# Expert blocks of a mixture-of-experts kernel: the down projection as three rounded products, ScalarE's and VectorE's order rewritten, row numbers copied ahead on GpSimd

## The chip, the cores and the metric

One core of one Trainium2 chip runs the whole program. The time is the device time of one launch in microseconds (us); the kernel's figure is the median of its runs.

## What is computed

One layer of a diffusion backbone on 1152 tokens of width 1024: an mLSTM and a gated linear recurrence, an output projection, and then a mixture of 64 small SwiGLU experts with 8 experts per token and one shared expert. Only this last part is touched. Cut to what matters:

```python
# 9216 (token, expert) entries sorted by expert, each expert padded to blocks of 128 rows
def expert_block(args):
    tok, e = args                      # 128 row numbers, one expert
    xb = x2d[tok]                      # (128, 1024)
    hb = jax.nn.silu(xb @ exp_w1[e]) * (xb @ exp_w3[e])     # (128, 256)
    return hb @ exp_w2[e]              # (128, 1024), the down projection

routed = jax.ops.segment_sum(yb * slot_w, slot_tok, num_segments=N)   # rows added back
shared = (jax.nn.silu(x2d @ shared_w1) * (x2d @ shared_w3)) @ shared_w2
return routed + shared
```

## The kernel before

`stage_experts` runs one loop over blocks of 128 rows. Blocks 0 to 8 (NSH = 9) are the shared expert over all tokens, read and stored with plain transfers. Then a loop, two blocks per turn, goes over the routed blocks, each with its expert and its list of row numbers; there are 106 of them with this input. Expert weights lie in three slots (WSLOT = 3): `w13` (2 MB per expert, inside the large tile `big`) and `w2` (1 MB, down weights). SyncE issues their transfers as slots come free, which it learns from semaphores.

There is no scheduler: each engine's order is written out by hand, and engines meet at semaphores.

- TensorE, for block b: `turn_h(b)` (two transposes of the hidden rows, line L1805), `up(b+1)` (24 products, L1798), `turn(b+2)` (8 transposes of gathered rows, L1785), `down(b)` (L1819). Up weights and tokens are each split into a rounded part (`wuph`, `xTh`, type fp32r) and a rest (`wupl`, `xTl`), and a product is made of three: high by high, high by rest, rest by high. `down` uses plain fp32, two products per half, on `hT` and `w2`.
- ScalarE: `ht(b)` copies the turned hidden rows out of the bank (L1879), `high(b+2)` rounds the up weights in two instructions (L1894), `silu(b+1)` (L1875), `xt(b+2)` makes `xTh` (L1868, L1869), `y_half(b)` copies the result to `y` (L1884, L1885), of which there are two buffers.
- VectorE: `low(b+2)` subtracts, giving `wupl` (L1956, two instructions), `hidden(b+1)` makes `hb` (L1946), `x_low(b+2)` makes `xTl` (L1965, two).
- GpSimd: `gather(b+4)` fetches rows into `xg` by an indirect transfer (L1719), `scatter(b)` adds `y` to `yacc` in memory by an indirect transfer (L1735). Both need row numbers in a small tile, `idx_g` or `idx_s`, copied on GpSimd by `tokens` (L1703), which first loads a column number (L1579). Each scatter waits until the one before has landed (`hold(scattered, ...)`), since both add to the same memory; the notice that a `y` buffer is free again (`scatter_done`, L1732) stands behind that wait.

## Time and profile before

| | |
|---|---|
| time, median of 3 runs | 2206.14 us (2202.48 to 2206.25) |
| the profiled execution: its own time, its span | 2207.35 us, 2205.5 us |
| busy share: TensorE, its weight loads, VectorE, ScalarE, GpSimd | 89%, 60%, 56%, 46%, 32% |
| first and last transpose of hidden rows (L1805) | 912.1 us, 2130.3 us |
| DMA in the expert stage, 920 to 2140 us | 233 GB/s, 0.72 of the queues' time |
| TensorE's granted clock in that stretch | 1.00 of full speed |

Busy times are a first guide only. In a pipeline of five engines with orders written by hand, what sets the pace shows in the distance from one block's start to the next and in which wait ends last.

### The profile page before, as it was taken

How to read it: one execution, taken by the hardware profiler on the slowest of the kernel's cores; microseconds unless marked ns; L12 is line 12 of the kernel's file. 1: busy time of each engine (PE TensorE's matmuls, PEld its weight loads, DVE VectorE, ACT ScalarE, POOL GpSimd, SP SyncE). 2: the span in 40 equal slices, each digit the busy share in tenths (PEclk: the TensorE clock that was granted, in tenths of full speed). 3: DMA queues.
4: the chain of work that ended last, by engine and by line, in shares of the span. 5: the costliest groups of instructions: out<-in, count | busy, mean ns of one | idle time of the engine just before them, and what ended most of it. 6: DMA issues, size and time to landing. Idle time of an engine off the chain costs nothing. (4 is left out here: it accounts for less than half of the span.)

```text
span 2205.5 us, 31257 instructions
## 1 busy us (share of the span) xinstructions
PE 1971.0 (89%) x8581; PEld 1323.5 (60%) x8582; DVE 1226.5 (56%) x1818; ACT 1025.4 (46%) x1478; POOL 710.6 (32%) x764
## 2 busy tenths in 40 slices
PE   5778998999998897699999999999999999999980
PEld 2344444568886444567677666667666666666650
DVE  2376444001777688766556555565655555555555
ACT  3355442101234111556566556566656556555652
POOL 4121000000013044433443454444444444454441
PEclk8899999999999998799999999999999999999995
DMA  8642101100003324347857888865667777777844
GB/s 264 216 164 86 39 19 48 38 20 20 11 1 134 139 82 149 134 148 260 303 160 231 289 292 273 266 195 139 180 205 253 268 266 263 255 267 266 278 112 171
DMA packets 108984, 380.62 MB, mean 173 GB/s; under 512 B 28413, under 2 KB 42749, under 8 KB 83965
## 3 DMA queue, kind: packets, MB, share of 16 engines
q1 hardware_dynamic: 62508, 261.05, 32.1%
q0 software_dynamic: 46128, 118.81, 20.8%
q8 instruction: 33, 0.54, 0.1%
q14 instruction: 25, 0.20, 0.0%
q10 hardware_dynamic: 290, 0.02, 0.0%
HBM read 336.59 MB, written 81.45 MB: 190 GB/s over the span
## 5 line engine op out<-in xcount | busy, mean ns | idle before, releaser
L1956 DVE TENSOR_TENSOR wupl<-big,wuph 128x2048 fp32r<-128x2048 f32 x234 | 525.9, 2289 | 494.9 <-ACT wuph L1894 460.5
L1894 ACT ACTIVATE wuph<-big 128x2048 fp32r (+1 forms) x234 | 435.8, 1917 | 7.1 <-SPq L1639 4.6
L1819 PE MATMUL bank<-w,hT 128*128 (+1 forms) x920 | 417.5, 596 | 0.7 <-issue 0.6
L1798 PE MATMUL bank<-wuph,xTh 128*128 128x512 f32 x928 | 373.2, 402 | 17.7 <-DVE xTl L1965 17.3
L1798 PE MATMUL bank<-wuph,xTl 128*128 128x512 f32 x928 | 365.4, 394 | 0.0
L1798 PE MATMUL bank<-wupl,xTh 128*128 128x512 f32 x928 | 364.0, 392 | 0.0
L1819 PEld LDWEIGHTS bank<-w,hT 128*128 128x128 f32 x920 | 166.6, 191 | 170.2 <-issue 169.9
L1719 POOL DMA_INDIRECT xg<-hn_scratch,idx_g x110 | 205.7, 1870 | 97.4 <-POOL idx_g L1703 91.1
L1884 ACT ACTIVATE y<-bank 128x512 f32<-128x512 f32 x115 | 68.8, 598 | 345.3 <-PE bank L1819 179.7
L1735 POOL DMA_INDIRECT yacc_scratch<-y,idx_s x106 | 177.7, 1676 | 110.5 <-ACT y L1885 59.2
L1798 PEld LDWEIGHTS bank<-wuph,xTh 128*128 128x128 f32 x928 | 176.2, 190 | 56.3 <-issue 22.4
L1798 PEld LDWEIGHTS bank<-wuph,xTl 128*128 128x128 f32 x928 | 174.9, 189 | 37.6
L1798 PEld LDWEIGHTS bank<-wupl,xTh 128*128 128x128 f32 x928 | 175.5, 189 | 34.3
L1703 POOL COPY idx_s<-shared 128x1 int32 x106 | 34.4, 324 | 415.7 <-DMA yacc_scratch<-y,idx_s 409.8
L1965 DVE TENSOR_TENSOR xTl<-bank,xTh 128x512 fp32r<-128x512 f32 x234 | 150.1, 683 | 17.3 <-ACT xTh L1869 17.3
L1785 PE MATMUL bank<-cst,xg 128*128 128x128 f32 x936 | 127.7, 280 | 35.5 <-DMA xg<-hn_scratch,idx_g 18.1
L1703 POOL COPY idx_g<-shared 128x1 int32 x110 | 151.1, 1374 | 15.8 <-PE bank L1785 10.4
L1785 PEld LDWEIGHTS bank<-cst,xg 128*128 128x128 f32 x936 | 122.0, 193 | 53.2 <-DMA xg<-hn_scratch,idx_g 27.4
L1246 PE MATMUL bank<-big,yT 128*128 128x512 f32 x288 | 130.9, 613 | 8.7 <-DMA big<-in_router_bias 8.7
L1195 DVE SCALAR_TENSOR_TENSOR eb<-bank,cols,cst 128x128 f32<-128x128 f32 x72 | 20.3, 344 | 156.7 <-PE bank L1062 156.7
L994 POOL TENSOR_SCALAR ml_ss<-ml_ss 128x4 f32<-128x4 f32 x8 | 1.6, 194 | 322.6 <-ACT big L1142 303.2
L1868 ACT ACTIVATE xTh<-bank 128x512 fp32r<-128x512 f32 x117 | 70.0, 598 | 68.8 <-PE bank L1785 65.4
(347 smaller groups left out, 2521.5 us busy)
## 6 DMA issues: line engine op xcount, KB each, us to landing
big<-in_exp_w SPq DMA_DIRECT2D x128, 1024.0 KB
w<-in_exp_w SPq DMA_DIRECT2D x64, 1024.0 KB
wada<-in_w_ada POOLq DMA_DIRECT2D x16, 1024.0 KB, 6.4
wada<-in_w_ada SPq DMA_DIRECT2D x4, 2048.0 KB, 11.9
wg<-in_w_in SPq DMA_DIRECT2D x8, 1024.0 KB, 5.6
x<-x_scratch SPq DMA_DIRECT2D x9, 512.0 KB
x_scratch<-x SPq DMA_DIRECT2D x9, 512.0 KB, 4.3
hn_scratch<-hn SPq DMA_DIRECT2D x9, 512.0 KB
```

The source lines that it names most:

```text
L1246: mm = pe.matmul(m.banks[2 + 2 * (t % 2) + half][:, :], m.yT[:, k, t * P:(t + 1) * P], m.wo[:, k, half * 512:(half + 1) * 512], start=(k = ...
L1703: pool.tensor_copy(dst[:, :], m.slots[:, bass.ds(c, 1), 0:1].rearrange("p c w -> p (c w)")).then_inc(listed, 1)
L1719: pool.indirect_dma_start(xg[j][:, :], None, m.hn2, bass.IndirectOffsetOnAxis(ap=idx_g[j][:, :], axis=0), bounds_check=N - 1, oob_is_err=F ...
L1735: pool.indirect_dma_start(m.yacc, bass.IndirectOffsetOnAxis(ap=idx_s[:, :], axis=0), y[j][:, :], None, compute_op=ALU.add, bounds_check=N ...
L1785: mm = pe.transpose(b_turn[k // 4][:, (k % 4) * P:(k % 4 + 1) * P], xg[j][:, k:D:KT], m.ident)
L1798: mm = pe.matmul(b_up[j][:, :], x[:, k, :], w[:, :, k, :], start=(k == 0 and i == 0), stop=(k == KT - 1 and i == 2))
L1819: mm = pe.matmul(b_down[half][:, :], hT[:, i, :], w2[:, at, i, half * 512:(half + 1) * 512].rearrange("p s n -> p (s n)"), start=(i == 0), ...
L1868: act.activation(xT[j][0][:, 0:4, :], b_turn[0][:, :].rearrange("p (k n) -> p k n", k=4), ACT.Copy)
L1884: act.activation(y[j][:, 0:512], b_down[0][:, :], ACT.Copy)
L1894: act.activation(part13(wup[j][0], half), raw13(e % WSLOT, half), ACT.Copy).then_inc(w_high, 1)
L1956: dve.tensor_tensor(part13(wup[j][1], half), raw13(e % WSLOT, half), part13(wup[j][0], half).bitcast(F32), ALU.subtract).then_inc(w_low, 1)
L1965: ins = dve.tensor_tensor(xT[j][1][:, 4 * i:4 * i + 4, :], b_turn[i][:, :].rearrange("p (k n) -> p k n", k=4), xT[j][0][:, 4 * i:4 * i + 4 ...
```

## The change

1. `down` becomes three rounded products per part, as `up` has: `hT` and the down weights are each split into a high part and a rest (`hT5h`, `hT5l`, `wdnh`, `wdnl`), 12 products in place of 4. The down weights are split anew for every block: `down_part` on ScalarE, `down_rest` on VectorE. There is one buffer of each, so both wait for the `down` before. `h_rest` on VectorE makes `hT5l`.
2. ScalarE's order: first half of the up weights, `wdnh`, `ht`, second half, the `y` of the block before, `silu`, `xt`. VectorE's order likewise.
3. GpSimd copies both lists of row numbers before it issues the gather; `idx_s` now has two buffers.
4. SyncE frees a slot of `w2` at `down_low`, which counts the rest parts. `hs` and `hb` move into an unused part of `big`.

```diff
-        idx_g, idx_s = [sb(f"idx_g{j}", [P, 1], I32) for j in range(2)], sb("idx_s", [P, 1], I32)
-        hs, hb = [sb(f"hs{j}", [P, DE]) for j in range(2)], [sb(f"hb{j}", [P, DE]) for j in range(2)]
-        hT = sb("hT5", [P, 2, P])
+        idx_g, idx_s = ([sb(f"idx_{n}{j}", [P, 1], I32) for j in range(2)] for n in "gs")
+        hs, hb = ([m.tail[:, (2 * i + j) * DE:(2 * i + j + 1) * DE] for j in range(2)] for i in range(2))
+        hT = [sb(f"hT5{part}", [P, 2, P], F32R) for part in "hl"]
+        wdn = [sb(f"wdn{part}", [P, 2, D], F32R) for part in "hl"]
...
-                sp.wait_ge(down_done, ends(e - WSLOT, r))
+                sp.wait_ge(down_low, 2 * ends(e - WSLOT, r))
...
-            def tokens(q, dst, step):
+            def tokens(q, dst):
 
                 c = column(pool, q)
                 pool.tensor_copy(dst[:, :], m.slots[:, bass.ds(c, 1), 0:1].rearrange("p c w -> p (c w)")).then_inc(listed, 1)
-                hold(listed, step)
...
-            def gather(q, j, loads, step):
+            def list_rows(q, j, loads):
 
                 hold(gathered[j], loads * 16)
+                tokens(q, idx_g[j])
+
+            def gather(q, j, step):
+
+                hold(listed, step)
                 hold(turned, q + (NSH - 1))
-                tokens(q, idx_g[j], step)
                 pool.indirect_dma_start(xg[j][:, :], None, m.hn2, bass.IndirectOffsetOnAxis(ap=idx_g[j][:, :], axis=0),
                                         bounds_check=N - 1, oob_is_err=False).then_inc(gathered[j], 16)
...
             def scatter(q, j):
                 hold(scattered, (q + NSH) * 16)
                 pool.sem_inc(scatter_done, 1)
-                tokens(q, idx_s, 2 * q + 6)
                 hold(y_act, q + (NSH + 2))
-                pool.indirect_dma_start(m.yacc, bass.IndirectOffsetOnAxis(ap=idx_s[:, :], axis=0), y[j][:, :], None,
+                pool.indirect_dma_start(m.yacc, bass.IndirectOffsetOnAxis(ap=idx_s[j][:, :], axis=0), y[j][:, :], None,
                                         compute_op=ALU.add, bounds_check=N - 1, oob_is_err=False).then_inc(scattered, 16)
...
-                    gather(r * 2 + (u + 4), j, r + (NSH + 4 + u) // 2, (r * 2 + (u + 4)) * 2 - 3)
+                    list_rows(r * 2 + (u + 4), j, r + (NSH + 4 + u) // 2)
+                    tokens(r * 2 + u, idx_s[j])
+                    gather(r * 2 + (u + 4), j, (r * 2 + u) * 2 + 6)
                     scatter(r * 2 + u, j)
...
-            def down(b, j, q=None):
-                if q is None:
-                    e, at = 0, slice(0, 1)
-                else:
-                    e = expert(pe, q)
-                    at = bass.ds(e % WSLOT, 1)
-                pe.wait_ge(w2_ready, e + 1)
-                pe.wait_ge(ht_ready, b + 1)
+            def down(b):
+                pe.wait_ge(down_high, 2 * b + 2)
+                pe.wait_ge(down_low, 2 * b + 2)
                 pe.wait_ge(y_act, b + 1)
+                (hh, hl), (wh, wl) = hT, wdn
                 for half in range(2):
+                    c = slice(half * 512, (half + 1) * 512)
                     for i in range(2):
-                        mm = pe.matmul(b_down[half][:, :], hT[:, i, :],
-                                       w2[:, at, i, half * 512:(half + 1) * 512].rearrange("p s n -> p (s n)"),
-                                       start=(i == 0), stop=(i == 1))
+                        for n, (h, w) in enumerate(((hh, wh), (hh, wl), (hl, wh))):
+                            mm = pe.matmul(b_down[half][:, :], h[:, i, :], w[:, i, c], start=(i == 0 and n == 0), stop=(i == 1 and n == 2))
                 mm.then_inc(down_done, 1)
...
-                act.activation(hT[:, :, :], b_h[:, 0:DE].rearrange("p (i n) -> p i n", i=2), ACT.Copy).then_inc(ht_ready, 1)
+                act.activation(hT[0][:, :, :], b_h[:, 0:DE].rearrange("p (i n) -> p i n", i=2), ACT.Copy).then_inc(down_high, 1)
+
+            def down_part(b, q=None):
+
+                e = 0 if q is None else expert(act, q)
+                act.wait_ge(w2_ready, e + 1)
+                if not (isinstance(b, int) and b == 0):
+                    act.wait_ge(down_done, b)
+                act.activation(wdn[0][:, :, :].rearrange("p i n -> p (i n)"), raw2(e % WSLOT), ACT.Copy).then_inc(down_high, 1)
...
-            def high(b, j, q=None):
+            def high(b, j, part, q=None):
 
                 e = 0 if q is None else expert(act, q)
-                act.wait_ge(w_ready, e + 1)
-                if not (isinstance(b, int) and b < 2):
-                    act.wait_ge(up_done, b - 1)
-                for half in HALVES:
-                    act.activation(part13(wup[j][0], half), raw13(e % WSLOT, half), ACT.Copy).then_inc(w_high, 1)
+                if part == 0:
+                    act.wait_ge(w_ready, e + 1)
+                    if not (isinstance(b, int) and b < 2):
+                        act.wait_ge(up_done, b - 1)
+                half = HALVES[part]
+                act.activation(part13(wup[j][0], half), raw13(e % WSLOT, half), ACT.Copy).then_inc(w_high, 1)
...
                     b, j = r * 2 + (u + NSH), (u + NSH) % 2
+                    high(r * 2 + (u + NSH + 2), j, 0, r * 2 + (u + 2))
+                    down_part(b, r * 2 + u)
                     ht(b)
-                    high(r * 2 + (u + NSH + 2), j, r * 2 + (u + 2))
+                    high(r * 2 + (u + NSH + 2), j, 1, r * 2 + (u + 2))
+                    y_half(r * 2 + (u + NSH - 1), 1 - j)
                     silu(r * 2 + (u + NSH + 1), 1 - j)
                     xt(r * 2 + (u + NSH + 2), j)
-                    y_half(b, j)
+            y_half(n * 2 + (NSH - 1), (NSH - 1) % 2)
...
-            def low(b, j, q=None):
+                dve.scalar_tensor_tensor(hb[j], hs[j], weight, b_up[j][:, DE:2 * DE], ALU.mult, ALU.mult).then_inc(h_done, 1)
+
+            def low(b, j, part, q=None):
 
                 e = 0 if q is None else expert(dve, q)
-                dve.wait_ge(w_ready, e + 1)
-                if not (isinstance(b, int) and b < 2):
-                    dve.wait_ge(up_done, b - 1)
-                for i, half in enumerate(HALVES):
-                    dve.wait_ge(w_high, 2 * b + (i + 1))
-                    dve.tensor_tensor(part13(wup[j][1], half), raw13(e % WSLOT, half),
-                                      part13(wup[j][0], half).bitcast(F32), ALU.subtract).then_inc(w_low, 1)
+                if part == 0:
+                    dve.wait_ge(w_ready, e + 1)
+                    if not (isinstance(b, int) and b < 2):
+                        dve.wait_ge(up_done, b - 1)
+                half = HALVES[part]
+                dve.wait_ge(w_high, 2 * b + (part + 1))
+                dve.tensor_tensor(part13(wup[j][1], half), raw13(e % WSLOT, half),
+                                  part13(wup[j][0], half).bitcast(F32), ALU.subtract).then_inc(w_low, 1)
+
+            def down_rest(b, q=None):
+
+                e = 0 if q is None else expert(dve, q)
+                dve.wait_ge(w2_ready, e + 1)
+                if not (isinstance(b, int) and b == 0):
+                    dve.wait_ge(down_done, b)
+                dve.wait_ge(down_high, 2 * b + 1)
+                dve.tensor_tensor(wdn[1][:, :, :].rearrange("p i n -> p (i n)"), raw2(e % WSLOT),
+                                  wdn[0][:, :, :].rearrange("p i n -> p (i n)").bitcast(F32), ALU.subtract).then_inc(down_low, 1)
+
+            def h_rest(b):
+
+                dve.wait_ge(down_high, 2 * b + 2)
+                dve.tensor_tensor(hT[1][:, :, :], b_h[:, 0:DE].rearrange("p (i n) -> p i n", i=2),
+                                  hT[0][:, :, :].bitcast(F32), ALU.subtract).then_inc(down_low, 1)
...
+                    low(k * 2 + (u + NSH + 2), j, 0, k * 2 + (u + 2))
+                    down_rest(k * 2 + (u + NSH), k * 2 + u)
+                    h_rest(k * 2 + (u + NSH))
+                    low(k * 2 + (u + NSH + 2), j, 1, k * 2 + (u + 2))
                     hidden(k * 2 + (u + NSH + 1), 1 - j, k * 2 + (u + 1))
                     x_low(k * 2 + (u + NSH + 2), j)
```

ScalarE, one block of the routed loop, before (names are tiles: `hs` is the silu output, `bank` a PSUM bank):

```order
L1884 ACTIVATE y<-bank 128x512
L1885 ACTIVATE y<-bank 128x512
L1879 ACTIVATE hT<-bank 128x256
L1579 ISA
L1579 TENSOR_LOAD tab
L1579 ISA x2
L1890 REGISTER_ALU
L1894 ISA
L1894 ACTIVATE wuph<-big 128x2048
L1894 ISA
L1894 ACTIVATE wuph<-big 128x2048
L1875 ACTIVATE hs<-bank 128x256
```

The same place after the change, from the second load of an expert's number on (`big` is now `hs`):

```order
L1893 ACTIVATE wdnh<-w 128x2048
L1885 ACTIVATE hT5h<-bank 128x256
L1581 TENSOR_LOAD tab
L1581 ISA x2
L1909 ISA
L1909 ACTIVATE wuph<-big 128x2048
L1898 ACTIVATE y<-bank 128x512
L1899 ACTIVATE y<-bank 128x512
L1881 ACTIVATE big<-bank 128x256
L1871 REGISTER_ALU
L1874 ACTIVATE xTh<-bank 128x512
L1875 ACTIVATE xTh<-bank 128x512
```

The `y` copies moved from ahead of `ht` to behind the second weight half, a new 128x2048 instruction stands ahead of `ht`, and the first weight half went behind the `xTh` copies of the turn before.

GpSimd, one block of the routed loop, before (`shared` holds the lists of rows, `tab` the columns' numbers):

```order
L1703 COPY idx_g<-shared 128x1
L1697 ISA
L1719 DMA xg<-hn_scratch,idx_g 128x1024
L1697 ISA
L1579 ISA
L1579 TENSOR_LOAD tab
L1579 ISA x2
L1703 ISA
L1703 COPY idx_s<-shared 128x1
L1697 ISA
L1697 REGISTER_ALU
L1735 DMA yacc_scratch<-y,idx_s 1280x1024
```

And after:

```order
L1708 COPY idx_g<-shared 128x1
L1581 ISA
L1581 TENSOR_LOAD tab
L1581 ISA x2
L1708 ISA
L1708 COPY idx_s<-shared 128x1
L1702 ISA
L1702 REGISTER_ALU
L1727 DMA xg<-hn_scratch,idx_g 128x1024
L1702 ISA
L1702 REGISTER_ALU
L1742 DMA yacc_scratch<-y,idx_s 1280x1024
```

The load of the column and the copy of `idx_s` moved from behind the wait for the last scatter's landing to ahead of the gather.

VectorE, one block after the change; before it was the two `wupl` in a row, then `hb` and the two `xTl`:

```order
L1991 TENSOR_TENSOR wdnl<-w,wdnh 128x2048
L1996 REGISTER_ALU
L1997 TENSOR_TENSOR hT5l<-bank,hT5h 128x256
L1581 TENSOR_LOAD tab
L1581 ISA x2
L1980 REGISTER_ALU
L1981 ISA
L1981 TENSOR_TENSOR wupl<-big,wuph 128x2048
```

Between the two `wupl` there are now `wdnl` and `hT5l`.

## Rows read from the trace of the kernel before

**Rows 1.** Window: length; busy PE, PEld, DVE, ACT, POOL; clock, DMA share, GB/s.

```profile
920.00:2140.00 1220.00, 1174.71 (x4801) 821.30 (x4799) 711.35 (x640) 732.66 (x916) 543.97 (x457) 1.00 0.72 233
```

**Rows 2.** Source view of L1805: weight loads of `turn_h`, first and last start.

```profile
L1805 PEld LDWEIGHTS bank<-cst,hb x230: 194/196/222, 912.1 to 2130.3; 128*128 128x128 f32 x115
```

**Rows 3.** Timeline of TensorE, one quiet block: start, length, line, count.

```profile
1504.46 3.60 PE L1819 MATMUL bank<-w,hT 128*128 x8
1507.89 0.39 PE L1805 MATMUL bank<-cst,hb 128*128 128x128 f32 x2
...
1508.59 0.40 PE L1798 MATMUL bank<-wuph,xTl 128*128 128x512 f32 x1
...
1513.38 0.40 PE L1798 MATMUL bank<-wuph,xTl 128*128 128x512 f32 x1
...
1517.94 0.39 PE L1805 MATMUL bank<-cst,hb 128*128 128x128 f32 x2
```

**Rows 4.** Source views of L1732, L1703 and L1735 on GpSimd: min/median/max ns.

```profile
L1732 POOLq EVENT_SEMAPHORE  x106: 17/17/17, 1021.2 to 2148.8; - x106
...
L1703 POOL COPY idx_s<-shared x106: 180/186/2074, 1022.1 to 2149.6; 128x1 int32 x106
...
L1735 POOL DMA_INDIRECT yacc_scratch<-y,idx_s x106: 1606/1617/3463, 1023.3 to 2150.8; - x106
```

**Rows 5.** Waits from 1008 to 2155 us: total us, times, longest.

```profile
DVE wupl L1956 <- ACT wuph L1894: 435.2, 101, 8.9
POOL idx_s L1703 <- DMA yacc_scratch<-y,idx_s: 409.8, 84, 9.3
...
ACT y L1884 <- POOLq L1732: 161.5, 38, 7.3
```

**Rows 6.** The page's groups: count, busy us, mean ns, idle before.

```profile
L1703 POOL COPY idx_s<-shared 128x1 int32 x106 | 34.4, 324 | 415.7 <-DMA yacc_scratch<-y,idx_s 409.8
```

**Rows 7.** Timeline of GpSimd, three scatters, around 1520 us.

```profile
1514.25 1.76 POOL L1703 COPY idx_s<-shared 128x1 int32 x1 [3.55 <-DMA yacc_scratch<-y,idx_s]
1517.06 1.62 POOL L1735 DMA_INDIRECT yacc_scratch<-y,idx_s  x1 [1.05 <-issue]
...
1519.74 1.05 POOL L1719 DMA_INDIRECT xg<-hn_scratch,idx_g  x1 [0.86 <-POOL idx_g L1703]
1524.21 1.84 POOL L1703 COPY idx_s<-shared 128x1 int32 x1 [3.43 <-DMA yacc_scratch<-y,idx_s]
1527.02 1.62 POOL L1735 DMA_INDIRECT yacc_scratch<-y,idx_s  x1 [0.97 <-POOL idx_s L1703]
...
1538.83 0.18 POOL L1703 COPY idx_s<-shared 128x1 int32 x1 [8.05 <-DMA yacc_scratch<-y,idx_s]
```

**Rows 8.** Windows of two scatters' flights: last columns clock, DMA share, GB/s.

```profile
1517.00:1523.00 6.00, 6.00 (x27) 4.58 (x26) 2.04 (x2) 4.86 (x5) 2.87 (x3) 1.00 0.66 123
1527.00:1538.00 11.00, 11.00 (x45) 7.55 (x44) 6.68 (x6) 6.44 (x8) 2.87 (x3) 1.00 0.99 328
```

**Rows 9.** Timelines of VectorE and ScalarE, the same quiet block.

```profile
1511.47 4.50 DVE L1956 TENSOR_TENSOR wupl<-big,wuph 128x2048 fp32r<-128x2048 f32 x2 [3.96 <-ACT wuph L1894]
...
1516.27 1.28 DVE L1965 TENSOR_TENSOR xTl<-bank,xTh 128x512 fp32r<-128x512 f32 x2
...
1508.09 0.60 ACT L1884 ACTIVATE y<-bank 128x512 f32<-128x512 f32 x1 [2.35 <-PE bank L1819]
...
1509.33 3.73 ACT L1894 ACTIVATE wuph<-big 128x2048 fp32r x2
```

**Rows 10.** Timeline of GpSimd, one scatter at 1310 us and what follows.

```profile
1310.57 1.62 POOL L1735 DMA_INDIRECT yacc_scratch<-y,idx_s  x1 [1.05 <-ACT y L1885]
1311.64 2.69 POOL L1703 COPY idx_g<-shared 128x1 int32 x1
1315.19 2.24 POOL L1719 DMA_INDIRECT xg<-hn_scratch,idx_g  x1 [0.86 <-POOL idx_g L1703]
```

**Rows 11.** Source view of L1719, the gathers.

```profile
L1719 POOL DMA_INDIRECT xg<-hn_scratch,idx_g x110: 1047/2204/3005, 983.6 to 2142.1; - x110
```

## Prediction before the changed kernel was run

> **What bounds the kernel now.** I read the busy times of the expert stage first [rows 1]. TensorE is busy in 1174.7 of 1220 us, so it looks like the bound. The starts of `turn_h` [rows 2] say otherwise: two records per block, 115 blocks, 114 steps from 912.1 to 2130.3 us, so 10.69 us per block, while an undisturbed block takes 1517.94 - 1507.89 = 10.05 us [rows 3]. Something else adds 0.64 us per block.
>
> The scatters give the name. There are 106, the first issued at 1023.3 and the last at 2150.8 us [rows 4], so 1127.5 / 105 = 10.74 us from one to the next: a little above the blocks' pace, and they are strictly serial, since each waits for the landing of the one before. GpSimd's copy of `idx_s` stands behind that landing and waits 409.8 us for it, and ScalarE's `y` copy waits 161.5 us for GpSimd's notice at L1732 that a `y` buffer is free [rows 5]. Those 161.5 us are the wait that ends last on average: ScalarE runs in order, so `hT`, the rounded weights and all that TensorE wants from them stand behind it. So the kernel has two near-equal bounds: TensorE's 10.05 us per block and the serial chain of scatters, 10.74 us, which wins.
>
> A step of that chain is a flight and a tail. The tail: L1732 runs at 1021.2 (last 2148.8), the `idx_s` copy at 1022.1 (2149.6), the scatter at 1023.3 (2150.8) [rows 4]. That is 0.85 us for loading the column number, then the copy, 0.32 us in the mean [rows 6], then 0.97 us to the scatter (1524.21 + 1.84 to 1527.02, [rows 7]). Sum 2.2 us, which leaves a mean flight of 10.74 - 2.2 = 8.5 us. One flight with little other traffic lasts 1524.21 - 0.85 - 1517.06 = 6.3 us, at 123 GB/s; the next one lasts 1538.83 - 0.85 - 1527.02 = 11.0 us, at 328 GB/s and a DMA share of 0.99 [rows 7, 8]. Between these two the mean of 8.5 means that some 47 in 100 flights are of the long sort, which meet the weights' transfers.
>
> **The change, part by part.**
> *TensorE.* The old down projection takes 1507.89 - 1504.46 = 3.43 us for four fp32 products, eight passes of 0.43 us. The rounded products of the up projection have the same shape and the same types as the twelve new ones: 21 steps from 1508.59 to 1513.38 us, 0.228 us each [rows 3]. Twelve take 2.74 us. The other end of the range would be a pass of fp32, 0.43 us, thus 5.15 us; nothing speaks for it with equal types. I take 2.74: a gain of 0.69 us per block, to 9.36 us.
>
> *ScalarE.* Added: `wdnh`, 128x2048, as one `wuph`: 3.73 us for two, 1.87 us [rows 9]. Its busy time per block is 732.7 / 1220 x 10.69 = 6.4 us [rows 1], then 8.3 us of 9.36. *VectorE.* Added: `wdnl`, as one `wupl`, 4.50 / 2 = 2.25 us [rows 9], and `hT5l`, 128x256, whose cost I bound by half of an `xTl` (1.28 / 4 = 0.32) and a whole one (0.64); I take 0.4. From 711.4 / 1220 x 10.69 = 6.2 us [rows 1] it goes to 8.9 of 9.36 us. Both still fit, with little left on VectorE.
>
> *Is a dependency late?* Counted from the start of `turn_h(b)`, up ends at about 6.1, turn at 7.0, down begins at 6.8 and ends at 9.7 us (the old distances with 0.69 taken off behind down). ScalarE: `xTh` at 7.0, the first `wuph` half of the block after next at 8.0, `wdnh(b+1)` at 9.8, which needs down(b) to have ended, as it just has. So `wdnh` runs from 0.45 to 2.35, `hT5h` to 2.6, second half to 4.4, `y` to 5.4, `hs` at 6.1. VectorE starts on the first half at 0.8, `wdnl` at 3.0, `hT5l` at 5.2 (ready at 5.7 for a down at 6.8), second half 5.6, `hb` 7.8, `xTl` 8.2 to 9.5. The next up begins at 9.7. That is 0 to 0.2 us of slack, where before `xTl` ended at 1516.27 + 1.28 = 1517.55 [rows 9] for an up right behind the `turn_h` at 1517.94 [rows 3], some 0.5 us. So the engines' own pace is 9.36 us at best; a bubble of 0.5 us on VectorE (each half now loads its expert's number itself) would cost at most that.
>
> *GpSimd.* Both row numbers are copied ahead of the landing. Of the tail the 0.85 and the 0.32 go; the 0.97 stays, plus 0.1 for two semaphore steps: 1.07 us. The chain's step is 8.5 + 1.07 = 9.57 us if flights stay as they are. They don't quite: scatters are then in flight for 8.8 of 9.9 us, 89% of the time, against 8.5 of 10.74, 79%, so they meet more of the same weight traffic, and the 2.2 us by which the mean exceeds 6.3 grows by 89/79 to 2.5. Step: 6.3 + 2.5 + 1.07 = 9.87 us. In long quiet stretches the chain could do 7.4 us but TensorE only 9.36; two `y` buffers carry part of that over, and I add 0.1: **9.95 us**. The copy of `y` now stands half a block later, at about 4.3 us of the next block, where before it stood at its very start (1508.09, [rows 9]), so a late scatter has some 3 us more before it stops ScalarE; this is what lets me add so little.
>
> *The sum.* 105 steps x (10.74 - 9.95) = 83 us. The eight shared-expert steps before them are on TensorE's pace: 8 x 0.69 = 5.5 us. `w2` slots come free a little earlier (`down_low` in place of `down_done`), which nothing waits for: the transfer queue waits for slots of the up weights. After the last block one `y` copy and one scatter remain, as before. Against the profiled execution's own time, 2207.35 us (span 2205.5), that is 2119 us; it stood 1.2 us above the median of the runs, so **2117 us**. No change can be told from one of under 0.2%, 4.4 us.
>
> **A lock that speaks against the change.** The copy of `idx_s` that began at 1514.25 took 1.76 us instead of its median 0.186 [rows 4, 7] and ended at 1516.01, where VectorE's `wupl` pair of 1511.47 + 4.50 ended [rows 9]. The gather, which can take 1.05 us, has a median of 2.20 us [rows 11]; in one held case the copy ahead of it took 2.69 and it 2.24 us [rows 10]. The Trainium skill (SBUF — State Buffer, "SBUF: two separate sides") says that a VectorE instruction with two SBUF inputs holds a port pair for its whole length against GpSimd's reads from SBUF. The trace agrees with it for these rows. `wdnl` is a third such instruction: 3 x 2.25 of 9.36 us, 72% of the time, against 2 x 2.25 of 10.05, 45%. What it can cost: scatter to end of gather took 1315.19 + 2.24 - 1310.57 = 6.9 us in the held case [rows 10] and 1519.74 + 1.05 - 1517.06 = 3.7 in the free one [rows 7]. A held second copy adds up to 2.25: 9.1 us, still in the shadow of a long flight, but above a short one.
>
> **Rivals.**
> 1. *The engines' loop is longer than 9.36* (the zero slack at `xTl`, held POOL work, or both): 1 us lost per block in each stretch that the flights don't rule, about half of it felt, gives 10.3 us: 105 x 0.44 = 46 us, **2160 us**. For it: VectorE at 95%. Against: its waits of 435.2 us for ScalarE [rows 5] show that its order is not tight now.
> 2. *The whole gain*: flights stay at 8.5 us and the later `y` takes up their spread, 9.45 us per step: 105 x 1.29 + 5.5 = 141 us, **2066 us**. For it: in the expert stage DMA moves 233 GB/s at a share of 0.72 [rows 1], with room. Against: the share of 0.99 in a long flight [rows 8].
> 3. *Slower, by the lock.* GpSimd's work between scatters becomes the chain's step. If every short flight is stretched to 9.1 + 1.07 = 10.2 us and the long ones stay at 11.0 + 1.07 = 12.0, the mean is 0.53 x 10.2 + 0.47 x 12.0 = 11.05: 0.3 us more than before, **2235 us**. It decides from a mean of 9.6 us for the short ones on; the free case, 7.4 us, is far from it, since a gap of VectorE's must be missed three times in each block.
> 4. *No change*: TensorE's gain isn't felt since flights lengthen by just what the tail gives up, 1.17 us. It takes a mean flight of 9.7 us.
>
> **Chances.** The forecast (2090 to 2145) 0.50; the whole gain 0.22; a longer loop 0.18; slower 0.06; no change 0.04. So faster 0.90, same 0.04, slower 0.06. The range is 2062 to 2168 us: from the whole gain to the longer loop.
>
> **What would show it.** Right: twelve down matmuls at 0.228 us; L1732's counterpart followed by the scatter within 1.1 us with no copy between; scatters 9.7 to 10.1 us apart; quiet blocks near 9.4 us; ScalarE's wait for the free `y` buffer well under 161 us. Wrong: quiet blocks at 10 us or more with TensorE waiting for `xTl` or `hT5l` (the loop), scatters waiting behind copies and gathers of 2 us each (the lock), or flights with a mean above 9.3 us (traffic).

## The result and the profile after

| | before | after |
|---|---|---|
| median of 6 runs, us | 2207.09 | 2184.99 (2179.75 to 2195.16) |
| ratio | | 0.9899, 95% interval 0.9878 to 0.9919 |
| span of the profiled execution, us | 2205.5 | 2193.3 |
| blocks 0 to 8 (shared expert), us | 96.8 | 109.3 |
| one routed block in the mean; a quiet one, us | 10.68; 10.05 | 10.46; 9.39 |
| from one scatter to the next, us | 10.74 | 10.50 |

The kernel is 1.0% faster, 22 us, where 89 were forecast. The time lies outside the range. (Some executions fall into a slower state: one each of e9, g8 and g10 below, 3019.9, 2203.2 and 2303.8 us, which the ratios leave out and the medians don't; without its slow run e9's median is 2154.3 us.) First the stage as a whole, by windows (columns as in [rows 1]):

```profile
920.00:2130.00 1210.00, 1114.18 (x5256) 918.78 (x5254) 1006.57 (x868) 939.38 (x1031) 657.25 (x458) 0.97 0.72 236
```

TensorE is now idle for 96 of 1210 us, VectorE's busy share went from 58% to 83%, and the traffic is what it was, 236 GB/s against 233. The source views that answer to [rows 2] and [rows 4] are those of `turn_h`, the notice and the scatter:

```profile
L1815 PEld LDWEIGHTS bank<-cst,big x230: 194/196/218, 911.3 to 2119.6; 128*128 128x128 f32 x115
...
L1740 POOLq EVENT_SEMAPHORE  x106: 17/17/17, 1034.2 to 2137.6; - x106
...
L1742 POOL DMA_INDIRECT yacc_scratch<-y,idx_s x106: 1600/2047/3682, 1036.5 to 2138.6; - x106
```

Step of the scatters: (2138.6 - 1036.5) / 105 = 10.50 us. The pace of the blocks is again that of the scatters. A quiet block, in TensorE's timeline as in [rows 3]:

```profile
1521.33 0.39 PE L1815 MATMUL bank<-cst,big 128*128 128x128 f32 x2
...
1527.86 0.47 PE L1827 MATMUL bank<-wdnh,hT5h 128*128 128x512 f32 x1
1528.17 0.39 PE L1827 MATMUL bank<-wdnl,hT5h 128*128 128x512 f32 x1
...
1530.72 0.39 PE L1815 MATMUL bank<-cst,big 128*128 128x128 f32 x2
```

1530.72 - 1521.33 = 9.39 us, and the twelve products of `down` with what starts them take 2.86. So TensorE's part of the change came out as forecast. The waits, which answer to [rows 5], show the price:

```profile
POOL yacc_scratch L1742 <- issue: 352.0, 102, 8.9
...
PEld bank L1795 <- DMA xg<-hn_scratch,idx_g: 95.8, 46, 6.0
...
DVE wupl L1981 <- ACT wuph L1909: 87.5, 106, 1.8
...
ACT y L1898 <- POOLq L1740: 16.6, 10, 3.5
```

ScalarE's wait for a free `y` fell from 161.5 to 16.6 us. In its place TensorE waits 95.8 us for gathered rows (before, 27). GpSimd's groups from 1008 us on (columns as in [rows 6]):

```profile
L1742 POOL DMA_INDIRECT yacc_scratch<-y,idx_s x106 | 243.2, 2294 | 370.7 <-issue 352.0 <-ACT y L1899 18.8
L1727 POOL DMA_INDIRECT xg<-hn_scratch,idx_g x108 | 203.8, 1887 | 113.4 <-issue 99.0 <-PE bank L1795 7.3 <-DMA yacc_scratch<-y,idx_s 5.2
...
L1708 POOL COPY idx_s<-shared 128x1 int32 x106 | 122.7, 1158 | 1.4 <-issue 1.1
```

These instructions make a transfer's descriptors, the list of pieces of memory that it moves; I call that time the generation. The scatter's went from 1.68 us in the mean (177.7 us for 106) to 2.29, and one of 3.60 us looks like this beside VectorE, in the timelines of the two engines:

```profile
1552.21 3.60 POOL L1742 DMA_INDIRECT yacc_scratch<-y,idx_s  x1 [1.55 <-issue]
1555.25 1.33 POOL L1708 COPY idx_g<-shared 128x1 int32 x1
...
1552.04 2.29 DVE L1981 TENSOR_TENSOR wupl<-big,wuph 128x2048 fp32r<-128x2048 f32 x1 [0.52 <-ACT wuph L1909]
1554.24 2.28 DVE L1991 TENSOR_TENSOR wdnl<-w,wdnh 128x2048 fp32r<-128x2048 f32 x1
1556.45 0.42 DVE L1997 TENSOR_TENSOR hT5l<-bank,hT5h 128x256 fp32r<-128x256 f32 x1
```

Laying every scatter from 1008 us on over VectorE's 128x2048 subtractions: the 11 that meet none for over 0.05 us take 1.61 us each, the 95 others 2.37 in the mean. Before, 64 met none (1.62) and 42 did (1.77). The gathers of after: 1.05 us without, 2.15 with.

Meeting a subtraction is not enough; the order of the two starts decides. In after, 67 scatters began while a subtraction had more than 0.1 us still to run, and each of them ended 1.45 to 1.53 us behind that subtraction's end. The 30 that began first, with a subtraction starting up to 1.6 us behind them, took 1.60 to 1.63 us. The kernel before had 4 scatters of the first kind (2.67 to 3.46 us) and 39 of the second (1.61 to 1.64 us; one met its subtraction for under 0.05 us). So the change did not only add a subtraction, it also moved the scatters' starts. The 106 generations of after take 72.9 us more than 1.606 us each: 50.4 of them under the old `wupl`, 22.5 under the new `wdnl`.

Taken apart scatter by scatter, by the records of each landing (105 steps; a flight runs from the scatter's start to its landing, the tail from the notice to the next scatter):

| us | before | forecast | after |
|---|---|---|---|
| flight | 8.37 | 8.8 | 9.11 |
| of it generation / the rest | 1.68 / 6.69 | | 2.29 / 6.82 |
| landing to notice, and tail | 2.37 | 1.17 | 1.39 |
| step | 10.74 | 9.95 | 10.50 |

### The profile page after: what moved, and what is told of

It is laid out like the page before. It is cut to its first block and busy times, and to the rows that moved or that the text cites. A ratio compares the mean times of both kernels' runs of the same rounds, so it can differ in the third digit from the quotient of the medians.

```text
span 2193.3 us, 33822 instructions
## 1 busy us (share of the span) xinstructions
PE 1910.1 (87%) x9041; PEld 1421.9 (65%) x9041; DVE 1525.1 (70%) x2048; ACT 1233.1 (56%) x1593; POOL 822.5 (38%) x764
## 5 line engine op out<-in xcount | busy, mean ns | idle before, releaser
L1981 DVE TENSOR_TENSOR wupl<-big,wuph 128x2048 fp32r<-128x2048 f32 x234 | 534.9, 2287 | 94.2 <-ACT wuph L1909 94.2
L1909 ACT ACTIVATE wuph<-big 128x2048 fp32r (+1 forms) x234 | 447.8, 1915 | 20.7 <-issue 11.4
L1742 POOL DMA_INDIRECT yacc_scratch<-y,idx_s x106 | 243.2, 2294 | 370.7 <-issue 352.0
L1991 DVE TENSOR_TENSOR wdnl<-w,wdnh 128x2048 fp32r<-128x2048 f32 x115 | 262.8, 2285 | 9.4 <-ACT wdnh L1893 9.4
L1893 ACT ACTIVATE wdnh<-w 128x2048 fp32r (+1 forms) x115 | 219.6, 1910 | 16.1 <-PE bank L1827 13.8
L1795 PE MATMUL bank<-cst,xg 128*128 128x128 f32 x936 | 135.3, 290 | 98.4 <-DMA xg<-hn_scratch,idx_g 76.4
L1827 PE MATMUL bank<-wdnh,hT5h 128*128 128x512 f32 x460 | 199.1, 433 | 9.5 <-issue 7.9
L1795 PEld LDWEIGHTS bank<-cst,xg 128*128 128x128 f32 x936 | 123.9, 195 | 124.4 <-DMA xg<-hn_scratch,idx_g 95.8
L1827 PE MATMUL bank<-wdnh,hT5l 128*128 128x512 f32 x460 | 188.9, 411 | 0.0
L1827 PE MATMUL bank<-wdnl,hT5h 128*128 128x512 f32 x460 | 187.2, 407 | 0.0
L1708 POOL COPY idx_g<-shared 128x1 int32 x110 | 167.8, 1526 | 5.9 <-issue 5.9
```

The lines of the kernel that those rows point to most:

```text
L1708: pool.tensor_copy(dst[:, :], m.slots[:, bass.ds(c, 1), 0:1].rearrange("p c w -> p (c w)")).then_inc(listed, 1)
L1742: pool.indirect_dma_start(m.yacc, bass.IndirectOffsetOnAxis(ap=idx_s[j][:, :], axis=0), y[j][:, :], None, compute_op=ALU.add, bounds_check ...
L1795: mm = pe.transpose(b_turn[k // 4][:, (k % 4) * P:(k % 4 + 1) * P], xg[j][:, k:D:KT], m.ident)
L1827: mm = pe.matmul(b_down[half][:, :], h[:, i, :], w[:, i, c], start=(i == 0 and n == 0), stop=(i == 1 and n == 2))
L1893: act.activation(wdn[0][:, :, :].rearrange("p i n -> p (i n)"), raw2(e % WSLOT), ACT.Copy).then_inc(down_high, 1)
L1909: act.activation(part13(wup[j][0], half), raw13(e % WSLOT, half), ACT.Copy).then_inc(w_high, 1)
```

## The experiments

Theory: VectorE's instructions with two inputs from SBUF (the memory on the chip that tiles lie in; a PSUM bank is the other place) hold up GpSimd, its descriptor generation too, so `wdnl` lengthens the serial chain. Rivals: denser blocks meet more traffic; the list copies ahead of the gather are at fault; the engines' own loop is. All times come from five rounds beside the kernel before. For each: the nine shared blocks, one routed block in the mean, the scatters' step, and the mean generation of scatter and gather.

| run | us | ratio | shared | block | step | generation |
|---|---|---|---|---|---|---|
| before | 2207.1 | | 96.8 | 10.68 | 10.74 | 1.68 / 1.88 |
| after | 2185.0 | 0.9899 | 109.3 | 10.46 | 10.50 | 2.29 / 1.89 |
| e1_pool_alone | 2144.8 | 0.9722 | 96.7 | 10.20 | 10.19 | 1.99 / 1.25 |
| e2_down_alone | 2313.8 | 1.0494 | 109.1 | 11.46 | 11.52 | 2.37 / 1.52 |
| e3_copies_behind_gather | 2187.6 | 0.9923 | 109.1 | 10.37 | 10.41 | 2.31 / 1.38 |
| e4_rest_from_psum | 2145.7 | 0.9732 | 109.3 | 10.09 | 10.11 | 2.13 / 1.85 |
| e5_spare_two_sbuf | 2152.5 | 0.9748 | 96.6 | 10.28 | 10.27 | 2.07 / 1.40 |
| e6_spare_from_psum | 2148.1 | 0.9724 | 96.5 | 10.15 | 10.15 | 1.90 / 1.23 |
| e7_after_two_sums | 2151.8 | 0.9744 | 112.1 | 9.92 | | 1.81 / 2.32 |
| e9_pool_two_sums | 2155.4 | 0.9759 | 101.2 | 10.07 | | 1.62 / 1.05 |
| g8_shared_split_once | 2175.4 | 0.9849 | 95.6 | 10.43 | 10.46 | 2.34 / 1.95 |
| g10_gather_first | 2100.0 | 0.9517 | 111.2 | 9.47 | | 2.80 / 1.87 |
| g11_first_and_once | 2090.7 | 0.9476 | 99.8 | 9.46 | | 2.85 / 1.88 |
| g12_no_sbuf_pairs | 2114.6 | 0.9597 | 109.5 | 9.73 | 9.73 | 1.61 / 1.05 |

Every interval is within 0.0034 of its ratio.

### The two halves of the change apart

e1_pool_alone is the kernel before with the change's GpSimd part only:

```diff
-                    gather(r * 2 + (u + 4), j, r + (NSH + 4 + u) // 2, (r * 2 + (u + 4)) * 2 - 3)
+                    list_rows(r * 2 + (u + 4), j, r + (NSH + 4 + u) // 2)
+                    tokens(r * 2 + u, idx_s[j])
+                    gather(r * 2 + (u + 4), j, (r * 2 + u) * 2 + 6)
```

> The kernel before with GpSimd's part of the change alone: both row numbers are copied ahead of the gather, idx_s has two buffers; the down projection and the other engines' orders stay. Lock theory (VectorE's instructions with two SBUF inputs hold GpSimd's copies, and what this delays is the gather): with only two such instructions per block there is room, the gather starts about 1 to 2 us later than before and has 13.8 us to land, so TensorE's wait for gathers stays near the 27 us of before, the scatters' tail falls from 2.27 to 1.25 us, their step from 10.74 to about 10.2 us: 2150 to 2170 us. Traffic theory (flights lengthen with the pace, wherever the copies stand): flights grow by what the tail gives up and the time stays at 2200 to 2210 us.

e2_down_alone is after with this part undone, and one `idx_s`.

> The changed kernel with GpSimd's code of before: idx_g is copied ahead of the gather, idx_s behind the landing of the last scatter. Lock theory: the gather is held by one copy only and starts earlier than in the changed kernel, but the scatters' tail is 2.3 us or more again; step 10.6 to 10.8 us, 2195 to 2215 us, with TensorE waiting for gathers for under 60 us instead of 96. Traffic theory: TensorE's wait for gathers stays at 90 us or more, the scatter's tail adds to it, 2215 to 2230 us.

Measured: 2144.8 us (interval of the ratio 0.9699 to 0.9746), 5 under the expected range, and 2313.8 us (1.0471 to 1.0517), which lies 99 us above the first theory's range and 84 above the second's. The GpSimd part alone gains 60 us or so and beats the whole change by 40; the split down projection alone costs 107. Its quiet blocks are 9.39 us here too, so it is not the engines' loop that costs. The waits of e2:

```profile
POOL idx_s L1708 <- DMA yacc_scratch<-y,idx_s: 433.2, 98, 8.7
PEld bank L1790 <- DMA xg<-hn_scratch,idx_g: 168.2, 48, 8.2
```

GpSimd waits for the landing in 98 of 106 blocks, so the chain is the bound: a step of 11.52 us, with a tail of 2.75 in place of 2.27 and a generation of 2.37 in place of 1.68. The gathers stand behind it, and TensorE waits 168 us for them. Flight less generation is the shortest of all runs here, 6.30 us.

In e1 the scatter's generation is already 1.99 us, without `wdnl`:

```profile
L1737 POOL DMA_INDIRECT yacc_scratch<-y,idx_s x106 | 211.4, 1994 | 411.3 <-issue 355.2 <-ACT y L1890 56.1
```

30 scatters took over 1.7 us, all begun under `wupl`, against 4 before. So moving the scatters' starts is enough to bring holds: the GpSimd part alone takes the generation from 1.68 to 1.99 us, the split alone to 2.37, both to 2.29. It costs e1 little, since its step of 10.19 us is near TensorE's own 10.05.

### The copies, and the rest from a bank

e3_copies_behind_gather keeps after, but a block's `idx_g` is copied a block ahead, so no copy stands between a scatter and the gather behind it:

```diff
-                    list_rows(r * 2 + (u + 4), j, r + (NSH + 4 + u) // 2)
+                    gather(r * 2 + (u + 4), j, (r * 2 + u) * 2 + 5)
                     tokens(r * 2 + u, idx_s[j])
-                    gather(r * 2 + (u + 4), j, (r * 2 + u) * 2 + 6)
+                    list_rows(r * 2 + (u + 5), 1 - j, r + (NSH + 5 + u) // 2)
```

> The changed kernel with both copies moved behind the gather (the gather's row numbers are then copied one block ahead). Lock theory: nothing that VectorE can hold stands ahead of the gather but its own start, so it is issued within 3 us of the scatter ahead of it instead of 5.1 in the mean, TensorE's wait for gathers falls from 96 to under 40 us, its clock no longer falls in most blocks, and the time is 2105 to 2140 us. Rival, late scatters (the gather is late since the scatter ahead of it waits for a y that comes half a block later, whatever the copies do): the wait for gathers stays above 80 us and the time within 5 us of 2185. Traffic theory: the gather starts earlier but its flight grows by as much; same time, 2180 to 2190 us.

The gather starts 2.6 us behind the scatter, not 5.1, yet TensorE still waits 79 us for gathers and the time is that of after: 2187.6 us, where the theory expected 2105 to 2140 and both rivals the time of after. The place of the copies alone is not the cause.

e4_rest_from_psum leaves out the true rest of the routed blocks' down weights: `wdnl`'s second input is a PSUM bank.

```diff
-                dve.tensor_tensor(wdn[1][:, :, :].rearrange("p i n -> p (i n)"), raw2(e % WSLOT),
-                                  wdn[0][:, :, :].rearrange("p i n -> p (i n)").bitcast(F32), ALU.subtract).then_inc(down_low, 1)
+                    rest = m.banks[0][:, :].unsqueeze(1).to_broadcast([P, 4, 512])
...
+                dve.tensor_tensor(out, raw, rest, ALU.subtract).then_inc(down_low, 1)
```

> The changed kernel, where in the routed blocks the instruction that writes the rest of the down weights takes its second input from a PSUM bank instead of from SBUF. It subtracts the wrong numbers, so it leaves out the true rest of the down weights; its length stays about 2.2 us and every order and wait is the same. Lock theory: a GpSimd copy that begins under it isn't held by it, the gather in quiet blocks starts 2 us earlier, the wait for gathers falls to 40 to 70 us and the time to 2140 to 2170 us. If VectorE's load as such, or the order, makes the gathers late: 2185 within 5 us.

2145.7 us, 39 less than after and within the theory's range, with an instruction of the same shape and length on VectorE (2.28 us). The 21 scatters and 26 gathers that began under it took no longer than free ones. Generation falls only to 2.13 us, since `wupl` still holds it; the tail falls from 1.25 to 1.06 us.

### The suspected cost added, and its control

To e1_pool_alone is added, at the end of VectorE's row of each routed block:

```diff
+                    twice = spare[:, :].unsqueeze(1).to_broadcast([P, 2, 1024])
+                    dve.tensor_tensor(spare_out[:, :].rearrange("p (k n) -> p k n", k=2), twice, twice, ALU.subtract).then_inc(spared, 1)
```

> The GpSimd change alone (e1_pool_alone, 2144.8 us, 10.19 us from scatter to scatter), plus, in every routed block, one spare 128x2048 subtraction on VectorE, both inputs from SBUF, put behind xTl at the end of its row, where VectorE has idle time (its row is about 7 us of the 10.05). Nothing else uses its result. Theory (such an instruction holds the scatter's own descriptor generation): generation goes from 1.99 us towards 2.3 and more, the step to 10.4 to 10.8, the time to 2170 to 2210. Rival (after's longer flights come from something else that the split brings, such as DMA traffic or later loops): as e1_pool_alone, 2135 to 2155.

> Control for e5_spare_two_sbuf: the same spare 128x2048 subtraction at the same place, with its second input from a PSUM bank. Theory (only two inputs from SBUF hold the generation): generation 2.0 us, time 2135 to 2155. Rival (any extra VectorE instruction costs, by its length in the row): the same time as e5_spare_two_sbuf, 2170 or more.

By their times this pair says little: 2152.5 and 2148.1 us, a difference of 4 within the intervals. e5 was expected at 2170 to 2210 and fell into its rival's range. The spare instruction runs right behind `xTl`, where few generations lie. But where one does lie there, the traces tell the two apart. Scatters whose generation met only the spare instruction by over 0.5 us: 15 in e5, 2.57 us in the mean; 20 in e6, 1.61 us each and none longer. Those that began first don't count, as they are free in both (5 in e5, 7 in e6, all 1.60 to 1.61 us). Of those that began under the spare instruction, the 10 of e5 took 2.02 to 3.74 us and the 13 of e6 1.60 to 1.61. Two of e5, the first held and the second ahead of the spare instruction, then one of e6, by their timelines:

```profile
1301.89 3.03 POOL L1739 DMA_INDIRECT yacc_scratch<-y,idx_s  x1 [6.27 <-issue]
...
1301.16 2.28 DVE L2047 TENSOR_TENSOR spare_out<-spare 128x2048 f32<-128x2048 f32 x1
```

```profile
1290.44 1.61 POOL L1739 DMA_INDIRECT yacc_scratch<-y,idx_s  x1 [4.78 <-issue]
...
1291.10 2.28 DVE L2047 TENSOR_TENSOR spare_out<-spare 128x2048 f32<-128x2048 f32 x1
```

```profile
1298.41 1.61 POOL L1739 DMA_INDIRECT yacc_scratch<-y,idx_s  x1 [7.17 <-issue]
...
1297.75 2.28 DVE L2047 TENSOR_TENSOR spare_out<-spare,bank 128x2048 f32<-128x2048 f32 x1
```

The first begins 0.73 us into the spare instruction and ends 1.5 us behind it. The last begins 0.66 us into its own, which reads a bank, and runs as if alone.

### The cost taken away

g12_no_sbuf_pairs does to both halves of `wupl` what e4 did to `wdnl`; the true rests of the routed blocks are left out.

```diff
+                    dve.tensor_tensor(quarters(part13(wup[j][1], half)), quarters(raw13(e % WSLOT, half)),
+                                      m.banks[0][:, :].unsqueeze(1).to_broadcast([P, 4, 512]), ALU.subtract).then_inc(w_low, 1)
```

> After, with the second input of every 128x2048 subtraction of the routed blocks (the rests of the up weights and of the down weights) from a PSUM bank. It leaves out the true rests; the instructions keep their shape and length, and the scatters still wait for one another. Theory (the longer step of the chain and GpSimd's late gathers come from VectorE's instructions with two inputs from SBUF): descriptor generation 1.61 and 1.05 us in every block, list copies of about 0.1 us, a step of 8.4 + 1.2 = 9.6 us or less, 2185 - 105 x 0.9 = 2090, range 2070 to 2110. Rival (the flight is longer because of traffic in denser blocks): the generation short but the step 10 us or more, 2130 and more.

GpSimd's groups, as for after:

```profile
L1742 POOL DMA_INDIRECT yacc_scratch<-y,idx_s x106 | 170.2, 1606 | 594.1 <-issue 466.7 <-ACT y L1899 127.4
L1727 POOL DMA_INDIRECT xg<-hn_scratch,idx_g x107 | 111.9, 1046 | 112.4 <-issue 109.4 <-PE bank L1795 3.0
```

Every generation is at its floor, with VectorE busy for 89% of the routed stretch (83% in after). The step is 9.73 us: a flight of 8.29 and 1.44 for notice and tail. In 23 steps the tail runs over its usual 1.0 us because the scatter waits for `y` from ScalarE, that is for TensorE: 36 us in all, 0.34 per step. The routed blocks take 1021.6 us (the 105 from block 9 to 113), against 1098.8 in after and 1070.6 in e1. So the hold costs after 77 us. How much the split is worth once the hold is gone shows best against e9 below, whose blocks run at TensorE's pace without it: 1057.8 us, 36 more. The time, 2114.6 us, is 25 above the 2090 of the sum, 5 above the theory's range and 15 below the rival's; the step, under 10 us, is the theory's. 14 us are the step, 0.13 us over the expected 9.6 by that wait for `y`, and 10 that the profiled execution of after, from which the sum's steps came, took 2195.2 us, 10 above its median. Flight less generation is 6.68 us, as before (6.69): with blocks at 9.73 us there is no longer flight from traffic, and that rival falls.

### The chain taken away

e7_after_two_sums lets even and odd blocks add to two sums in memory, with a semaphore each; a scatter waits for the one before the last. The second sum is cleared early and added in the last stage.

```diff
+            def landed(j, loads):
+                hold(scattered[j], loads * 16)
+                pool.sem_inc(scatter_done, 1)
...
             def scatter(q, j):
-                hold(scattered, (q + NSH) * 16)
-                pool.sem_inc(scatter_done, 1)
                 hold(y_act, q + (NSH + 2))
+                acc = (m.yacc, m.yacc2)[j]
...
+                    landed(j, r + (NSH + u) // 2)
                     list_rows(r * 2 + (u + 4), j, r + (NSH + 4 + u) // 2)
```

> After, with the scatters of even and odd blocks going to two sums in memory, so that a scatter waits for the landing of the one before the last and no longer for the last. The second sum is cleared early and added in the last stage (9 more VectorE instructions of 1.23 us, about 12 us at the end). Theory (the chain of serial scatters is what bounds after, at 10.50 us): the blocks fall to TensorE's 9.39 us or a little over (9.4 to 9.6), 105 x 1.0 less and 12 more, 2075 to 2110. Rival (GpSimd's own row, held by VectorE, or TensorE's late gathers bound it as much): 2150 to 2190.

> The GpSimd change alone with the same two sums. TensorE's 10.05 us bounds the blocks either way: 2144.8 - 105 x 0.13 + 12 = 2143, range 2125 to 2155. If after with two sums (e7) is below this by about 60 us, the split of the down projection is worth what its TensorE time says once the chain is gone; if not, the split costs more on the other engines than it saves.

e7 missed its range: 2151.8 us, the rival's. e9, 2155.4 us, came out at the upper end of its range. TensorE is busy there without a gap, at 10.05 us in a quiet block and 10.07 in the mean; the second sum makes it start and end later. e7's blocks are 9.92 us, since GpSimd's row became the bound:

```profile
1519.84 1.61 POOL L1749 DMA_INDIRECT yacc_scratch<-y,idx_s  x1 [0.31 <-issue]
1524.88 0.48 POOL L1711 COPY idx_g<-shared 128x1 int32 x1 [3.43 <-issue]
1525.63 1.93 POOL L1711 COPY idx_s<-shared 128x1 int32 x1 [0.27 <-issue]
1528.59 2.38 POOL L1730 DMA_INDIRECT xg<-hn_scratch,idx_g  x1 [1.03 <-ACT y L1910]
```

The list copies stand behind the landing of the scatter two back (3.43 us of idling), and the gather behind both, 8.75 us after the scatter. TensorE waits 58.7 us for it. g10_gather_first puts list and gather ahead of that wait:

```diff
-                    landed(j, r + (NSH + u) // 2)
                     list_rows(r * 2 + (u + 4), j, r + (NSH + 4 + u) // 2)
+                    gather(r * 2 + (u + 4), j, (r * 2 + u) * 2 + 5)
+                    landed(j, r + (NSH + u) // 2)
                     tokens(r * 2 + u, idx_s[j])
-                    gather(r * 2 + (u + 4), j, (r * 2 + u) * 2 + 6)
+                    hold(listed, (r * 2 + u) * 2 + 6)
```

> After with two sums (e7_after_two_sums, 2151.8 us, where TensorE waits 59 us for gathers and GpSimd's list copies wait for the landing of the scatter two blocks back), with the gather and its list ahead of that wait. Theory (with the chain gone, GpSimd's row is the bound, since its gather stands behind the landing and two held copies): the gather starts some 3 us earlier, TensorE's waits for it fall under 20 us, the time by 35 to 55 us, 2095 to 2120. Rival (flights and held generation bound it in any order, as moving the copies alone showed in e3_copies_behind_gather): 2140 to 2155.

```profile
1521.90 1.68 POOL L1749 DMA_INDIRECT yacc_scratch<-y,idx_s  x1 [4.50 <-issue]
1523.05 0.73 POOL L1711 COPY idx_g<-shared 128x1 int32 x1
1524.83 2.54 POOL L1730 DMA_INDIRECT xg<-hn_scratch,idx_g  x1 [1.05 <-issue]
```

The gather now follows the scatter by 2.9 us, TensorE's wait for it is no longer in the list of waits, and a block takes 9.47 us: 2100.0 us (0.9503 to 0.9530), within the theory's range. Against e9 the split gains 55 us, near the 105 x 0.66 = 69 of the quiet blocks less the 10 that the shared blocks lose. The scatter's generation is longer than ever, 2.80 us in the mean, and costs nothing, for nothing serial stands behind it.

### The shared blocks

In g8_shared_split_once block 0 alone splits the shared expert's down weights; for blocks 1 to 8 both engines keep their waits and go on:

```diff
+                if q is None and b >= 1:
+                    act.sem_inc(down_high, 1)
+                    return
```

> After, with the down weights of the shared expert split once, for block 0, and not again for the eight blocks that use the same weights; ScalarE and VectorE keep their waits there and pass on. Theory (the nine shared blocks are 12.5 us longer than before because the list work on VectorE now stands ahead of a 2.3 us rest that the next down projection needs): the first nine blocks fall from 109 us to 97 or less, the time by 10 to 14 us, 2171 to 2178. Rival (only the engines' new order in these blocks costs, not the repeated split): no change, 2180 to 2190.

The shared blocks fall from 109.3 to 95.6 us and the time by 10: 2175.4. The cause shows on VectorE, in after, where work on the token lists is put between the blocks (the first row is its start):

```profile
920.60 0.18 DVE L1280 TENSOR_SCALAR big<-big 128x64 f32<-128x64 f32 x1
...
926.39 2.29 DVE L1981 TENSOR_TENSOR wupl<-big,wuph 128x2048 fp32r<-128x2048 f32 x1
928.60 2.28 DVE L1991 TENSOR_TENSOR wdnl<-w,wdnh 128x2048 fp32r<-128x2048 f32 x1
930.81 0.41 DVE L1997 TENSOR_TENSOR hT5l<-bank,hT5h 128x256 fp32r<-128x256 f32 x1
```

Behind 5.8 us of list work `hT5l`, for which `down` waits, is ready at 931.2 us. In g8 the same `hT5l` is ready at 926.4:

```profile
923.81 2.29 DVE L1984 TENSOR_TENSOR wupl<-big,wuph 128x2048 fp32r<-128x2048 f32 x1
926.01 0.42 DVE L2003 TENSOR_TENSOR hT5l<-bank,hT5h 128x256 fp32r<-128x256 f32 x1
```

Blocks 1 and 3, which meet list work, took 10.5 and 10.8 us before, 15.2 and 17.7 in after, and 11.4 and 12.1 in g8. Block 6 took 14.0, 17.5 and 13.5 us; there TensorE waits 6.3 us for a plain load of rows, which GpSimd issues late, and why it is later in after was not followed up. TensorE's waits in these blocks cost twice, as its clock falls (912 to 1012 us, after and then g8; the clock is the third from the end, and was 0.98 before):

```profile
912.00:1012.00 100.00, 83.16 (x377) 68.09 (x376) 83.43 (x124) 65.28 (x74) 36.49 (x37) 0.91 0.36 127
```

```profile
912.00:1012.00 100.00, 92.64 (x446) 76.67 (x445) 78.87 (x126) 63.06 (x80) 34.40 (x39) 0.98 0.47 170
```

g11_first_and_once has both edits:

> Both together: two sums, gather first, the shared down weights split once. The sum of the two: 12 us below g10_gather_first, 2083 to 2110. If the first blocks' gain is lost later (the routed blocks start sooner but wait for something else), it equals g10_gather_first.

2090.7 us, ratio 0.9476 (0.9461 to 0.9490), with nothing of the computation left out: the fastest version, 94 us under after. It comes in 9 us under g10, as expected within what the runs can tell.

## Why the prediction was wrong, point by point

The forecast was right in its parts outside the chain. TensorE: 9.39 us for a quiet block where 9.36 was worked out. The hand-laid rows of ScalarE and VectorE: no bubble, although VectorE is busy for 8.60 us of 9.39 in the quiet block shown above. The wait for a free `y`: 16.6 us left of 161.5. The bound named, the serial chain of scatters, is still the bound, and taking it away (e7, g10) shows it. Rivals 1 and 2 did not happen. Rival 4 asked for a mean flight of 9.7 us; it was 9.11, and not by traffic.

The span was to fall by 88.5 us and fell by 12.2. The 76 missing lie in two places. (By the medians of all runs 67 are missing, as the profiled execution of after was 10 us above its median.)

**105 x (10.50 - 9.95) = 58 us in the step of the chain.** The failed step is the paragraph "GpSimd", and behind it "A lock that speaks against the change". There I saw the hold in the copies and the gather, priced their row at up to 9.1 us, and let it hide behind a long flight. I took the scatter's own generation as free of it, because its median of 1.617 us in [rows 4] looked like a constant. The maximum of 3.463 us in the same row said otherwise: 4 scatters of before were held, and 39 escaped by starting just ahead of a subtraction, an order that the change, with new rows on every engine, did not keep. A flight begins with its generation: 1.68 us became 2.29, which is 0.61 us in each of 105 serial steps, 64 us. That is rival 3 by its mechanism, at another place than I put it: not the row between scatters, but the scatter itself. To this comes 0.22 us in the tail, where e4 shows a part of `wdnl`'s hold (1.25 to 1.06 us). The trace of after shows the rest: 24 tails are over 1.2 us, and in 19 of them the scatter starts 0.30 or 0.31 us behind the end of the gather, which ended behind the notice. In sum the flight is 0.31 us and the tail 0.22 us over the forecast. My term for traffic, +0.3 us of flight for denser blocks, did not show at this pace: flight less generation is 6.69 us before, 6.82 after and 6.68 in g12; only e2, with a step of 11.52 us, has less, 6.30. It hid half of what the generation added. The flight it was added to was itself 0.13 us too long: 8.5 us by the rows, 8.37 by the landings.

**12.5 + 5.5 = 18 us in the shared blocks.** The step "The eight shared-expert steps before them are on TensorE's pace: 8 x 0.69" failed. It took the layout of a quiet block for all nine, and overlooked that VectorE's rows of blocks 0, 2 and 3 also hold list work, behind which every new instruction stands. g8 gives 13.7 us of it back.

The hold also has a second price, which I had not seen at all: a late gather makes TensorE wait (95.8 us in all), though the chain would in part have ruled there anyway, and how much of the 96 us is felt is left open. It is not the gather's place alone: in e1 it starts 5.1 us behind its scatter, as in after, and TensorE waits 1.4 us.

The Trainium skill (SBUF — State Buffer, "Who interferes with whom") says that a VectorE instruction with two inputs from SBUF contends with GpSimd instructions that read SBUF, and infers that descriptor generation is spared, as it needs the write side. For the list copies the trace agrees: the 78 copies of `idx_g` in after that began under such an instruction ended 0.04 or 0.05 us behind it. For the generation of these indirect transfers it does not, and the measurement decides: 1.61 us became up to 3.68 beside such instructions, and stayed at 1.61 beside those with one input from PSUM. Whether it is the reading of `idx_s` that is held was not tried. That a held generation always ends some 1.5 us behind the subtraction, nearly its whole free length, says only that the hold falls at its start.

## What to carry to other kernels

Before VectorE work with two SBUF inputs is added beside GpSimd transfers, lay the existing generations over VectorE's timeline and compare the held with the free ones: minimum, median and maximum of the row, not the median alone. Look at the order of starts, too: a generation that starts just ahead of a subtraction is free, but a new order may move it under one. A chain that bounds the kernel pays for every such hold, and generation that nothing serial waits for cost nothing in g10, so break the chain first (two sums, and the gather ahead of the wait for a landing): the same split of the down projection cost 40 us on top of the GpSimd change and gained 55 once that was done. And a rest of weights that don't change from block to block is made once.

## What the runs showed of the hardware

A scatter's descriptor generation, 1.61 us alone, lasted up to 3.68 us in after where it began under a subtraction of 2.29 us with two SBUF inputs, and ended 1.45 to 1.53 us behind that subtraction (67 scatters); begun ahead of one, it took 1.60 to 1.63 us (30 scatters). A gather's, 1.05 us alone, took 2.15 in the mean where it met one. A list copy took 0.17 to 0.78 us where it met none, and up to 4.97 us in after. With the second input from PSUM, at the same length on VectorE, every generation was at its floor (g12: 1.578 to 1.645 us for all 106 scatters, 1.046 in the mean for the gathers), and the copies took at most 0.78 us.

TensorE's clock fell after its own waits. In after it waited for gathered rows from 1904.11 to 1907.55 us; the windows before that wait, of the `down` behind it, and later:

```profile
1890.00:1904.00 14.00, 14.00 (x67) 11.46 (x65) 12.25 (x9) 11.96 (x14) 7.53 (x6) 1.00 0.62 198
1908.40:1913.10 4.70, 4.70 (x18) 3.77 (x17) 2.55 (x3) 2.88 (x3) 0.77 (x1) 0.64 0.95 375
1913.10:1920.00 6.90, 6.90 (x37) 5.87 (x36) 5.64 (x4) 5.68 (x7) 5.84 (x4) 1.00 0.81 195
```

The granted clock in that `down` was 0.64, between its two levels of 1.2 and 2.4 GHz, and the twelve products took 4.58 us instead of 2.9. In six more places of after between 1250 and 1990 us, behind waits of 3.0 to 5.6 us, `down` took 3.8 to 5.0 us.
